# A mixture-of-experts decoder layer: the place of the further passes is moved, and the last expert's rows are added up in PSUM

## The reference, cut to what matters

```
h = h + hierarchical_moe(rmsnorm(h, norm_ffn_w), ...)
# 4 groups x 8 experts; top-1 group, top-2 experts in it: 256 x 2 assignments
hidden = silu(xb @ w1[e]) * (xb @ w3[e])      # 2048 -> 512
ys     = hidden @ w2[e]                       # 512 -> 2048
out    = sum over the token's two experts of weight * ys
return rmsnorm(h, final_norm_w)[:, N_META:]
```

## Time and profile before

| | us |
|---|---|
| runs shown (three) | 1539.2 median, 1538.2 to 1540.98 |
| profiled execution, its own time | 1545.64 |
| its span, first to last instruction | 1543.9 |
| PE busy | 1292.5 (84%) |
| DVE, ACT, POOL busy | 430.1, 308.4, 41.8 |
| HBM read | 482.21 MB, 314 GB/s over the span |
| granted TensorE clock, mean | 0.906 |

### The profile page before, as it was taken

The page is one execution under the profiler, slowest core; times in us unless marked ns, Lnnn a source line. Parts: engine busy times, 40 slices in busy tenths (PEclk is TensorE's granted clock), DMA queues, the critical chain, the costliest instruction groups (busy, mean ns, idle before and its releaser), DMA issues.

```text
span 1543.9 us, 18242 instructions
## 1 busy us (share of the span) xinstructions
PE 1292.5 (84%) x7656; PEld 742.8 (48%) x7656; DVE 430.1 (28%) x1016; ACT 308.4 (20%) x469; POOL 41.8 (3%) x79
## 2 busy tenths in 40 slices
PE   6999999999999997878778768868868767768865
PEld 5788888778888884323223223223223223223221
DVE  3413543331321002534112212212212212312332
ACT  3202413112131011212112112112112112111103
POOL 3100000000000120000000000000000000000001
PEclk8999999999999998988878888888888889988886
DMA  6543344443455735999999999999999999999993
GB/s 174 181 129 109 110 117 135 151 147 109 134 166 218 272 110 231 422 434 433 432 428 430 435 432 430 430 432 434 433 430 430 434 433 434 428 430 435 433 424 159
DMA packets 104009, 485.06 MB, mean 314 GB/s; under 512 B 19708, under 2 KB 89624, under 8 KB 90904
## 3 DMA queue, kind: packets, MB, share of 16 engines
q1 hardware_dynamic: 101664, 478.65, 76.7%
q0 software_dynamic: 1024, 3.37, 0.7%
q10 hardware_dynamic: 1272, 2.32, 0.4%
HBM read 482.21 MB, written 2.12 MB: 314 GB/s over the span
## 4 chain that ended last, share of the span: by engine, by line
PE 55%; DMA 42%; DVE 1%; ACT 1%; issue 1%; ACTq 1%; DVEq 0%; SPq 0%
DMA big<-in_moe_w_dram 42%; PE bank L1322 25%; PE bank L1643 7%; PE bank L1374 7%; PE bank L1669 3%; PE bank L1682 3%; PE bank L1624 2%; PE bank L1653 1%; PE bank L1408 1%; PE bank L1387 1%; PE bank L1452 1%; PE bank L1631 0%; PE bank L1589 0%; PE bank L1381 0%; DVE big L1220 0%
## 5 line engine op out<-in xcount | busy, mean ns | idle before, releaser
L1643 PE MATMUL bank<-big 128*32 128x512 f32 x2048 | 303.7, 748 | 204.1 <-DMA big<-in_moe_w_dram 202.4
L1322 PE MATMUL bank<-big 128*128 128x272 f32 (+1 forms) x1664 | 383.1, 390 | 0.5 <-DVE colc L948 0.5
L1322 PEld LDWEIGHTS bank<-big 128*128 128x128 f32 x1664 | 315.1, 191 | 56.4 <-DVE colc L948 0.6
L1643 PEld LDWEIGHTS bank<-big 128*32 128x32 f32 x2048 | 75.8, 133 | 429.3 <-DMA big<-in_moe_w_dram 215.6
L1207 DVE COPY big<-bank 128x512 f32<-128x512 f32 x32 | 22.1, 692 | 544.7 <-PE bank L1643 544.7
L1220 DVE TENSOR_TENSOR big<-big,bank 128x512 f32<-128x512 f32 x256 | 156.0, 682 | 36.8 <-PE bank L1682 36.8
L1669 PE MATMUL bank<-big 128*32 128x512 f32 x1024 | 134.7, 673 | 0.9 <-DVE big L1212 0.9
L1682 PE MATMUL bank<-big 32*128 32x512 f32 x512 | 133.2, 633 | 1.5 <-ACT big L806 1.5
L1374 PE MATMUL bank<-big 128*128 128x256 f32 x512 | 113.9, 381 | 0.0
L1374 PEld LDWEIGHTS bank<-big 128*128 128x128 f32 x512 | 96.3, 190 | 12.6
L789 ACT ACTIVATE big<-bank 128x512 f32<-128x512 f32 x32 | 19.1, 597 | 383.0 <-PE bank L1624 383.0
(11 more groups left out here) (279 smaller groups left out, 721.7 us busy)
## 6 DMA issues: line engine op xcount, KB each, us to landing
big<-in_moe_w_dram SPq DMA_DIRECT2D x94, 4096.0 KB, 32.9
big<-in_w_in_dram SPq DMA_DIRECT2D x26, 2048.0 KB, 8.8
big<-in_w_out_dram SPq DMA_DIRECT2D x8, 2048.0 KB, 8.4
big<-in_moe_w_dram SPq DMA_DIRECT2D x4, 2048.0 KB, 18.8
big<-gate_rows POOLq DMA_DIRECT2D x8, 272.0 KB, 3.7
big<-in_x_dram SPq DMA_DIRECT2D x2, 1024.0 KB, 6.4
out_dram<-big SPq DMA_DIRECT2D x4, 512.0 KB, 3.2
big<-gate_rows POOLq DMA_DIRECT2D x2, 544.0 KB, 5.5
```

Of the source, the lines that this page charges most:

```text
L1322: last = V.matmul(outs, a, b, start=start and j == 0, stop=stop and j == n - 1)
L1643: last = V.matmul(pb[2 + r][CAP * g:CAP * (g + 1), :], xsT[:, j, g, :], w[:, 4 * g + j, :], start=j == 0, stop=j == 3)
```

## The change

Three things are changed together.

1. The further passes stand between experts 24 and 25 (`BREAK = 24`). Expert 24 ends without working ahead, all its sums are awaited, then come the passes, then expert 25 starts afresh and 26 to 31 follow in the pipeline, `tokens(31)` inside expert 30. PE now loops over experts 5 to 20 and unrolls 21 to 30. The passes count on semaphores of their own (`further_steps_pe`, `_act`, `_dve`, `further_in`), so the waits of the experts behind them don't contain `count`. `fw` is loaded there too.
2. The last w2 is loaded in halves of columns: half 0 gives columns 0 to 1023 of all tokens, half 1 the others. `h2` is brought into the banks by identity matmuls (`carried`), and `spread`, with 64 rows of `wT` and `ysb` at once, adds the expert's rows there. DVE's sums of the last expert are gone.
3. ACT squares the banks, DVE multiplies the banks by `fw` (`weighted`), the two taking turns on a pair of banks. POOL does nothing at the end. Of each token half ACT scales columns 1024 to 2047 and DVE 0 to 1023.

```diff
+        LAST_BANKS = ((0, 1, 2, 3), (6, 7, 4, 0))
+        EARLY = [(0, 0), (0, 1), (1, 0), (1, 1)]
+        LATE = [(0, 2), (0, 3), (1, 2), (1, 3)]
+        BREAK = 24
...
+        def columns_of(e, h):
+            return moe_w2[0, e, :, :].rearrange("(p k) (h c) -> p h k c", p=P, h=2)[:, h, :, :]
...
@@ SP
+            sp.wait_ge(s["ov_ready"], 1)
+            count = sp.value_load(ov_n[0:1, 0:1], min_val=0, max_val=NOV)
+            with sp.If(count > 0):
...
+            reached(sp, "y_ps", count, True)
+            for m in range(3 * BREAK + 4, 3 * NE - 1):
                 sp.wait_ge(used[(m - 4) % 3], (m - 4) // 3 + 1)
...
@@ ACT, the end
+            for h, order in ((0, EARLY), (1, LATE)):
+                act.wait_ge(s["y_ps"], NE + h)
+                V.activation(ysb, pb[5][:, :], ACT.Copy).then_inc(s["ys_ev"], 1)
+                for j in (1, 0, 3, 2):
+                    square(4 * h + j, *order[j])
+                    if h and j == 0:
+                        root(0)
+            scaled(0)
             root(1)
+            scaled(1)
@@ DVE, the end
+            dve.wait_ge(s["fw_in"], 16)
+            for h, order in ((0, EARLY), (1, LATE)):
+                for j in range(4):
+                    weighted(4 * h + j, *order[j])
+                    if h and j == 2:
+                        mean(0)
             inverse(0)
+            scaled(0)
             mean(1)
             inverse(1)
+            scaled(1)
@@ PE, the end
+            def carried(a, d):
+                V.matmul(pb[LAST_BANKS[a][d]][:, :], ident[:, :], h2[:, a, d * 512:(d + 1) * 512], start=True, stop=False)
...
+            def spread(a, d):
+                q = 64 * (d % 2)
+                V.matmul(pb[LAST_BANKS[a][d]][:, :], wT[q:q + 64, a * P:(a + 1) * P], ysb[q:q + 64, :],
+                         start=False, stop=True).then_inc(s["cb_ps"], 1)
+            n = NE - 1
+            up(n, [places(n)[0][0], places(n)[1][0]], [places(n)[0][1], places(n)[1][1]], 8 * (n - 1) + 5)
             turn_hidden(n)
+            pe.wait_ge(s["y_acc"], 8 * n)
+            for a, d in EARLY:
+                carried(a, d)
+            pe.wait_ge(s["hT_ready"], n + 1)
+            down_half(0)
+            for a, d in LATE[0:2]:
+                carried(a, d)
+            pe.wait_ge(s["wt_ev"], n + 1)
+            carried(*LATE[2])
+            pe.wait_ge(s["ys_ev"], n + 1)
+            for a, d in EARLY:
+                spread(a, d)
+            down_half(1)
+            pe.wait_ge(s["f_g"], 1)
+            pe.wait_ge(s["f_sq"], 2)
+            carried(*LATE[3])
+            pe.wait_ge(s["ys_ev"], n + 2)
+            for a, d in LATE:
+                spread(a, d)
```

More of the change, by code:

```diff
@@ L847, in root, with scaled @@
                     s["f_rms"], 1)
[L849 to L853, removed]
-            root(1)
[L855 to L859, removed]
+            def scaled(a):
+                act.wait_ge(s["f_rs"], a + 1)
+                act.wait_ge(s["f_g"], 4 * a + 4)
+                V.activation(fout[:, a, 1024:2048], fout[:, a, 1024:2048], ACT.Copy,
+                             scale=frs[:, a:a + 1]).then_inc(s["f_act"], 1)
+            for h, order in ((0, EARLY), (1, LATE)):
[6 more added lines that the diff above has]
+            scaled(0)
+            root(1)
+            scaled(1)
         @block.vector
@@ L1638, in up @@
                 for r in range(2):
-                    pe.wait_ge(m_in[slots[r]], counts[r])
+                    pe.wait_ge(m_in[slots[r]] if loaded is None else loaded, counts[r])
                     w = eslot(slots[r]).rearrange("p (k f) -> p k f", f=FE)
@@ L1710, in _ @@
                 one(n, places(n), settled=8 * (n - 2) + 5)
-            with pe.Fori(1, 7) as i:
+            with pe.Fori(1, 5) as i:
                 for q in range(1, 5):
                     one(i * 4 + q, [(j, i * 48 + c) for j, c in places(q)], settled=i * 32 + (8 * (q - 2) + 5))
-            one(29, places(29), settled=8 * 27 + 5)
-            one(30, places(30), ahead=False, settled=8 * 28 + 5)
+            for n in range(BREAK - 3, BREAK + 1):
+                one(n, places(n), ahead=n < BREAK, settled=8 * (n - 2) + 5)
@@ L1728, in _ @@
-            n = count + (NE - 1)
-            tokens(n)
-            turn_tokens(n)
-            up(n, [places(NE - 1)[0][0], places(NE - 1)[1][0]], [places(NE - 1)[0][1], places(NE - 1)[1][1]],
-               count * 8 + 8 * (NE - 1))
-            turn_hidden(n)
-            down(n, *places(NE - 1)[2], 32)
-            combine(n, banks=LAST_BANKS)
+                    n = i + 1
+                    tokens(n, True)
+                    turn_tokens(n, True)
+                    reached(pe, "y_acc", n, True, part=7, back=1)
@@ new lines, in _ @@
+                    up(n, [0, 0], [i * 48 + 16, i * 48 + 32], x=True, loaded=further_in)
+                    turn_hidden(n, x=True)
+                    down(n, 0, i * 48 + 48, x=True, loaded=further_in)
+                    combine(n, x=True)
+            reached(pe, "y_acc", count, True, part=7)
+            tokens(BREAK + 1)
+            turn_tokens(BREAK + 1)
+            one(BREAK + 1, places(BREAK + 1), before=False, settled=8 * (BREAK + 1))
+            for n in range(BREAK + 2, NE - 1):
+                one(n, places(n), settled=8 * (n - 2) + 5)
@@ new lines, in _, with down_half @@
+            combine(NE - 2)
+            def carried(a, d):
+                V.matmul(pb[LAST_BANKS[a][d]][:, :], ident[:, :], h2[:, a, d * 512:(d + 1) * 512], start=True, stop=False)
+            def down_half(h):
+                pe.wait_ge(m_in[3] if h == 0 else half_in, places(NE - 1)[2][1] if h == 0 else 32)
+                w = eslot(3).rearrange("p (h k c) -> p h k c", h=2, k=KF)
+                for ki in range(2):
+                    for g in range(QR):
+                        k = 2 * ki + g % 2
+                        last = V.matmul(pb[5][CAP * g:CAP * (g + 1), :], hTb[:, k * CAP:(k + 1) * CAP],
+                                        w[:, h, k, (g // 2) * 512:(g // 2 + 1) * 512], start=ki == 0, stop=ki == 1)
+                last.then_inc(s["y_ps"], 1)
```

319 lines of the change are left out of this document (168 added, 151 removed).

## The result

The changed kernel takes 1541.25 us (median of 20 runs, 1539.05 to 1545.49), the kernel before 1539.15 (20 runs on the same chip, 1534.4 to 1543.88). The ratio is 1.0019 [1.0011, 1.0028]: slower by 0.2%, some 2 to 3 us, and clear of the noise. I had predicted 1536.7, 2.5 us faster, and gave 0.17 to slower.

A forecast was written before the change was run, and what follows sets the result against it. The weight stream bounds the expert stage, the order of work around the branch the tail. Break gain 6.1 us, less a longer tail and later stores, left 3.0; 0.5 for clock left 2.5: 1536.7 from 1539.2, range 1533.5 to 1542.5.

The forecast's parts named there:

- I carry the difference over as it is: Whole kernel: the gain, summed on one profiled execution (run 1545.64), was applied unchanged to the median of 1539.2.
- The signs that I named for "right": Trace after: up(31) on w3 near 1507.4, no 3.8 us issue, short waits, 0.89 us carried sums, last compute near 1536.
- The new tail, 20.6: End of the last expert: from the turning to the last computation 20.6 us, against 17.9 in the kernel before.
- rival 1: Carried sums, 1515.5 to 1523.6: the clock stays low through them, costing 8.1 us more, 1544.8; chance 0.12.
- rival 2: spread in the last expert: 64-row matmuls do not pair, +1.78 early and +0.89 late, 1539.4; chance 0.13.
- `up(31)` on w3 at the low clock, 5.9: Last expert: PE idles 6 us for w3, then starts at the low clock and takes 5.9 us, to 1513.3.
- rival 4: Last expert: larger gain, squares begin earlier and up runs at full clock, 3.64 us for 5.9, 1534.3; chance 0.15.
- "Cost 0" for the break: Between experts 24 and 25: the moved break costs nothing, 8 to 11 us of cover before the weight stream waits.
- rival 3: Break at 24: its signals come later than the cover, stalling the stream 1 to 4 us, 1537.7 to 1540.7; chance 0.08.
- Column halves of w2: Last w2 load: 4 KB pieces for 16 KB cost nothing to 4.9 us more per half; 0 was taken.
- Squares and weights from the banks: Kernel's end: ACT squares and DVE rows alternate over two banks; first late pair to last computation 7.0 us, 1536.05.
- The rule on tiling modes: Six tiling changes from the turning to the last spread: no gap by the trace; by the rule 0.3 us less gain.

The follow-up runs named there:

- a_fwlate: The changed kernel with the load of fw put back to its old place, behind silu of expert 30: 1543.22 us, 1.0018 of the kernel before.
- best2: Passes at 24, old end, fw late, with up(31) waiting for five sums and POOL making four products: 1538.68 us, 0.9994 of the kernel before.
- p24_oldtail: The changed kernel with the end of the kernel before, further passes still between experts 24 and 25: 1538.24 us, 0.9993 of the kernel before.
- p24_old_fwlate: The changed kernel with the old end and the load of fw back behind silu of expert 30: 1537.44 us, 0.9982 of the kernel before.
- pause_only: Old end, fw late, pause kept between experts 24 and 25, without count reading, branches or further passes: 1538.0 us, 0.9987 of the kernel before.
- none_old: The kernel before without any further passes, tokens(31) ahead, fw at its old place, old tail: 1535.48 us, 0.9973 of the kernel before.

## Why the prediction was wrong, point by point

- **"I carry the difference over as it is"**: the step that failed. The sum was made on one execution, whose end was the slowest of eight and whose time lay 6.4 us above the median of the runs that I had in front of me; its 2.5 us were then taken off that median. That gap (1545.64 against 1539.2) was the warning, and I named it and passed it by. The excess sat in the very steps that the change moves or replaces: from the last one-hot to the end of `down(31)` the eight traces of before hold 28.3, 27.7 and 26.5 us, or 24.8, 23.3 and three times 22.0. Against the typical end the move gives 3.5 us, not 6.1: from the landing of w3 to the end of the turning it is 9.3 to 9.8 us in the four quickest traces (11.1 to 14.1 in the others), and 5.8 to 6.1 after. And the old tail up to the last computation is 16.2 us there (1515.07 to 1531.28), not 17.9. Left in the time of its own execution (1545.64 - 2.5) the sum would have said 1543.1, against 1541.2 of the profiled execution of the kernel after.
- **The sum with the right terms**: move -3.5, new tail 25.7 against 20.7, +5.0, w3 of expert 31 landing 1.5 us later behind m=73 (208.0 against 206.5): 3 us slower, from 236.7 to 239.6 in traces. Against the median of the eight ends, 237.8, it is 1.8 us. The timed runs give +2.1 (20 runs), and 1.8 to 2.7 by the repeats.
- **Ahead of my zero**, where the prediction has no term: from the landing of m=3 to that of m=73 it is 690.3 to 690.9 us in the eleven traces without the break at 24, and 691.1 to 691.6 in five of the nine with it. In the other four (the third trace of the kernel after is one) it is 693.7 to 694.6, with the first `up` at 9.59 to 9.63 us in place of 7.07. None of the eleven has that. So a part of the timed loss may lie there; why a break at 24 should touch the first expert is open, and the small number of traces leaves room for chance.
- **The signs that I named for "right"** came true nearly all (no "issue", no long wait, 0.87 us for each new matmul, a tail of 20.7), and the time was still wrong: each of them looks at the kernel after, none at the trace of before from which I subtracted.
- **The new tail, 20.6**: right, 20.7, in all six traces that have it. The carried sums took 3.44 and 2.77 (predicted 3.56 and 2.67), and the granted clock was 1.00 throughout: rival 1 didn't happen (nor does its arithmetic hold: 2.5 - 0.5 - 8.1 is -6.1, and the 5.6 is 2.5 - 8.1). I had written that the identity matmuls "eat nearly half of what the move gives"; they cost 4.7 us on the path, where the move gives 3.5.
- **`spread` with 64 rows (rival 2)**: 1.99 us for eight records, where 1.78 for two abreast was taken. They pair.
- **`up(31)` on w3 at the low clock, 5.9**: in the first trace PE didn't stand idle ahead of w3. It was busy with expert 30 until 1502.82, so w1 and w3 form one block of 8.67 us. The low clock fell on w1 (granted 0.50 from 1503 to 1506), and w3 took 3.62 us at the full one; the turning ended 1.7 us earlier than predicted, as rival 4 had it. In `a_fwlate`, where PE did wait 4.5 us for w3, it was 5.80.
- **"Cost 0" for the break (rival 3)**: wrong in its outcome and not as rival 3 had it. There is no PE wait over 6.5 us behind the break (4.2 at 1352.15, 6.0 at 1391.13), and reading the count and branching have no part. The premise that failed is that the slot "is wanted when the load three further on has landed", 29 us behind the landing: m=79 was issued 12.5 to 17.5 us behind the landing of m=75 whose slot it takes, well within that, and the stream lost 1.4 to 1.6 us. In the traces of before it is issued 3.7 to 5.4 us behind. In the kernel before the same pause comes when all loads have been issued, and costs the stream nothing.
- **Column halves of w2**: 0 was taken. The streams with them are some 0.3 us longer than those with row halves (218.0 against 217.7, 216.6 against 216.3), and the second half lands 6 us ahead of its use at 1523.74.
- **Squares and weights from the banks**: the first late pair is done some 1.0 us behind 1526.65 (half of the 1.93), 13.9 us behind the turning where 13.6 was predicted, and from it to the last computation it is 6.8, predicted 7.0. The forms of the kernel after, 1500 us to the end, show the prices, and those of DVE and ACT are within some 4% of the earlier trace rows:

```profile
L1813 PE MATMUL bank<-big 64*128 64x512 f32 x16 | 4.0, 615 | 0.0
L1799 PE MATMUL bank<-big,ident 128*128 128x512 f32 x16 | 7.6, 605 | 0.0
L1349 DVE TENSOR_TENSOR big<-bank,big 128x512 f32<-128x512 f32 x8 | 5.3, 689 | 11.5 <-PE bank L1813 10.2 <-ACT big L868 1.0
L868 ACT ACTIVATE big<-bank 128x512 f32<-128x512 f32 x8 | 4.7, 592 | 5.0 <-PE bank L1813 4.7
```

- **The rule on tiling modes**: between the turning, the carried sums, `down` and `spread` the chain has no gap at any of the six changes (1513.76 + 3.44 = 1517.20, 1519.05 + 2.77 = 1521.82, 1523.74). The Trainium skill (TensorEngine Tiling (Array Packing), Key Properties) says that a change of tiling mode drains TensorE; no drain is to be seen here. The ends of matmuls are modelled in these traces, so a short drain could hide.

## What to carry to other kernels

If the profiled execution's own time lies above the median of the runs by as much as the forecast gain, first find where it lost it; when that is the stretch the change touches, take the prices from a second and third profile. A wait removed is worth only what the next bound leaves: in the quick executions `down(31)` already began 0.3 to 0.8 us behind the last byte. Adding a residual in the banks by identity matmuls cost some 0.9 us of PE for each bank of 512 float32 columns, and here it freed nothing that was slower. Had PE been idle at that place it might have paid; no run tried it.

## What was not expected of the hardware

- One and the same program: behind a pause of PE the granted clock is 1.2 GHz in some executions and 2.4 GHz in others, and `up` takes 9.6 to 10.0 us, 7.07, or something between (8.37). It happened at `up(0)` and at `up(31)`, and a dip in the middle of dense work at `down(31)` (5.31 or 3.69), each by itself. The two groups in the timed runs of the kernel after (1539.0 to 1541.3 and 1543.0 to 1545.5) fit with the first; that is argued, not shown.
- The "issue" in front of `tokens(31)` was 3.79, 3.76, 3.15, 2.71, 0.71, 2.72, 3.54 and 2.75 us in eight executions.
- A slot given back 12.5 to 17.5 us behind its landing in place of 3.7 to 5.4, with two or three loads of 4 MB in flight, lengthened the stream by 1.4 to 1.6 us in each of nine traces (rows against row halves, columns against column halves). The slices of 38.6 us are too coarse to show it (430 GB/s in either kernel). Why is open.
- DVE's `scalar_tensor_tensor` over 1024 columns takes 1.28 us when POOL has finished (best2, form view). Beside POOL the two hinder each other, and only one of them pays. In all eight traces of the kernel before it took 2.40 to 2.43 us, and the last POOL product beside it its usual 1.26 to 1.27. In the four traces with the old end and the break moved or left out (`p24_oldtail`, `p24_old_fwlate`, `pause_only`, `none_old`) it began some 0.3 us ahead of POOL's last product; there it took 1.43 to 1.44, and that product 2.24 to 2.26. The second row is from the timeline of `p24_old_fwlate`:

```profile
L1361 DVE SCALAR_TENSOR_TENSOR big<-big,frs 128x1024 f32<-128x1024 f32 x2 | 2.5, 1284 | 0.0
```

```profile
1526.44 1.44 DVE L1360 SCALAR_TENSOR_TENSOR big<-big,frs 128x1024 f32<-128x1024 f32 x1
```
